# Two attentions of a fused block kernel: implied semaphore waits dropped, one wait moved, and products copied out 512 columns at a time

## The chip, the cores and the metric

The kernel runs on one core of one Trainium2 chip. The metric is the time on the device in microseconds (us) from one launch to its end. The engines are TensorE (PE, with its weight loads as PEld), VectorE (DVE), ScalarE (ACT), GpSimd (POOL) and the queue that issues the DMAs (SP). Each engine runs its own list of instructions in order, and they wait for each other by semaphores.

## The reference

Two layers follow each other on a sequence of 1024 tokens with 1024 features, all in float32. What the change touches is the two attentions, one in each layer:

```python
def one_block(qi):                       # first layer: 8 query heads, 2 key/value heads, width 64
    s = jnp.einsum('bqkgd,bskd->bkgqs', qi, k) * scale
    p = jax.nn.softmax(s, axis=-1)       # over all 1024 keys
    return jnp.einsum('bkgqs,bskd->bqkgd', p, v)

for blk in range(seqlen // ATT_BLOCK):   # second layer: 16 heads, width 64, causal
    q0, q1 = blk * ATT_BLOCK, (blk + 1) * ATT_BLOCK
    s = jnp.einsum('bhqd,bhkd->bhqk', q[:, :, q0:q1], k[:, :, :q1]) * scale
    s = s + fcum[:, :, q0:q1, None] - fcum[:, :, None, :q1]
    prob = jax.nn.softmax(jnp.where(kpos <= qpos, s, -jnp.inf), axis=-1)
    outs.append(jnp.einsum('bhqk,bhkd->bhqd', prob, v[:, :, :q1]))
```

Around them stand a gated token mixer, a gated feed-forward net with a short convolution, a state-space branch, and dense projections. Those are left as they are.

## The kernel before, in words

Every engine has a class with the same stages, and each stage walks the same steps, so that the order of an engine's work is the order of its own Python loop. A result is named by a label; `done(label)` lets the instruction raise its engine's one counter, and `wait_ge(*at(label))` waits for it. `wait_ge` leaves a wait out when this engine has already waited for a count of that semaphore at least as high (line 374 is where a wait is written, so every separate wait instruction has that line).

**One step of an attention.** The unit is a block of 128 queries of one head, numbered g. In the first attention there are 64 (eight heads of eight), and each sees 1024 keys. In the second there are 128: eight pairs p of heads with 16 blocks each, and block qt = g % 8 sees (qt + 1) * 128 keys. For one block the engines do this:

- PE `scores` (L805, L806): the query block against the high and the low part of the keys, 512 columns at a time into one of two PSUM tiles of 1024 columns. In the second attention a small matmul for the mask (L810) is last.
- DVE `top`: the maximum of each row (L2573); in the second attention a subtraction with maximum (L2568) and a change of sign (L2571, label `minus`).
- ACT `soft`: the exponential, with the row's sum (L1645). DVE `soft`: its reciprocal (L2581). POOL `weigh` (L3451, label `weighed`): the row times that reciprocal.
- PE `turn` (L829): transposes by 128 columns, four to a PSUM bank (bank 4 and bank 5). ACT `turn` (L1660, label `phi`) copies each bank out, rounded, as the high part; DVE `turn` (L2596, label `plo`) subtracts that from the bank and so makes the low part.
- PE `back` (L848), once for every two blocks (number n = g // 2): the values against the high and low parts, 256 columns, 16 matmuls in the first attention, into bank 6. Partitions 0 to 63 and 64 to 127 of the product are two partial sums. ACT `back` (L1668, label `outhi`) copies the first half out and DVE `back` (L2604, label `out`) adds the second to it.

**The order.** Step s of the first attention (s from -2 to 65) is, on PE: scores(s + 2), turn(s), and when s is even back(s - 1). On DVE: top(s + 2), the two subtractions of turn(s), reciprocal(s + 2), and when s is even the addition. On ACT: the two copies of turn(s), exponential(s + 2), and when s is even the copy of the product. On POOL: weigh(s + 2), and now and then an addition of squares. So "an even step" has a product at its end and "an odd step" has none.

In the second attention the steps are the same, but PE has other work between them. `self.fill(fills(p, s, True))` stands between scores(s + 2) and turn(s), and runs pieces of dense projections (three matmuls of 512 columns, L609 to L611, to a piece): none to three pieces a step. Their weights are split into a high part by ACT (L1393) and a low part by POOL (L3374), in POOL's one queue with `weigh`.

**Waits around the change.** `bank_free(b)` waits for the labels that the last user of bank b left in `emptied[b]`. For scores these are `top` and, in the first attention, `exp`; for the transposes `phi` and `plo` of the block that last used the bank; for the product `out`. PE waits for `weighed` of block g just ahead of the transposes of g, so in the second attention behind the pieces of dense work. At s == 22 of the first attention PE adds up the token mixer's squares into bank 7, and ACT takes the root.

Of the kernel before, what the change touches and what calls it, by code (L numbers as in the profile page):

```python
# [9 lines left out]
ACT = mybir.ActivationFunctionType  # L10
ALU = mybir.AluOpType
# [532 lines left out]


class TensorEngine(Engine):
    def __init__(self, K, op):
# [244 lines left out]

    def scores(self, A, g, h, qt, q, kh, kl, causal, ready):
        K = self.K
        nk = (qt + 1) * 128 if causal else 1024
        pair = g % 2
        qs = K.wrr(q)[:, qt * 128:(qt + 1) * 128]
        for half in range((nk + 511) // 512):
            c = slice(half * 512, min(nk, half * 512 + 512))
            out = K.ps[pair][:, c]  # L800
            diag = causal and c.stop == nk
            self.bank_free(2 * pair + half)
            for label in ready:
                self.wait_ge(*K.at(*label))
            self.op.matmul(out, qs, K.wrr(kh)[:, c], start=True, stop=False)  # L805
            t = self.op.matmul(out, qs, K.wrr(kl)[:, c], start=False, stop=not diag)  # L806
            if diag:
                self.consts()
                self.wait_ge(*K.at("maskr"))
                t = self.op.matmul(K.ps[pair][:, nk - 128:nk], K.idr[:, :], K.maskr[:, :],  # L810
                                   start=False, stop=True)
        t.then_inc(*self.done("scores", A, g))
        free = (("top", A, g),) if causal else (("top", A, g), ("exp", A, g))
        for half in range((nk + 511) // 512):
            self.emptied[2 * pair + half] = free

    def turn(self, A, g, qt, p, causal):
        K = self.K
        nk = qt + 1 if causal else 8
        par = g % 2 if nk <= 4 else 0  # L820
        self.consts()
        for half in range((nk + 3) // 4):
            bk = (half + par) % 2
            js = range(4 * half, min(nk, 4 * half + 4))
            self.wait_ge(*K.at("weighed", A, g))
            self.bank_free(4 + bk)
            for j in js:
                o = bk * 512 + (j - js[0]) * 128
                t = self.op.transpose(K.ps[2][:, o:o + 128], K.w(p)[:, j * 128:(j + 1) * 128],  # L829
                                      K.c_id)  # L830
            t.then_inc(*self.done("turn", A, g, half))
            self.emptied[4 + bk] = (("phi", A, g, half), ("plo", A, g, half))

    def back(self, A, g, qt, hi, lo, v, causal, ready):

        K = self.K
        nk = qt + 1 if causal else 8
        for gg in (g - 1, g):
            for half in range((((qt if gg == g else qt - 1) + 1 if causal else 8) + 3) // 4):
                self.wait_ge(*K.at("phi", A, gg, half))  # L840
                self.wait_ge(*K.at("plo", A, gg, half))
        for label in ready:
            self.wait_ge(*K.at(*label))
        self.bank_free(6)
        for j in range(nk):
            c0 = 128 if causal and j == qt else 0
            for n, m in enumerate((hi, lo)):
                t = self.op.matmul(K.ps[3][:, c0:256], K.wrr(v)[:, j * 128:(j + 1) * 128],  # L848
                                   m[:, j, c0:256], start=(j == 0 and n == 0),
                                   stop=(j == nk - 1 and n == 1))  # L850
        t.then_inc(*self.done("product", A, g // 2))
        self.emptied[6] = (("out", A, g // 2),)

    def attend1(self):
        K = self.K

        def sc(s):
            h, qt = s // 8, s % 8
            k = 8 if h < 4 else 10
            self.scores(1, s, h, qt, h, k, k + 1, False, (("stacklo", "q", h // 2), ("stacklo", "q", 4),  # L860
                         ("stackhi2", "q", 4, 1)))

        for s in range(-2, 66):
# [6 lines left out]
            if s >= 2 and s % 2 == 0:  # L870
                hi, lo, _ = pt1(K, ((s - 1) // 2) % 2)
                self.back(1, s - 1, (s - 1) % 8, hi, lo, 12 + (s - 1) // 32, False,
                          (("vstack", 1),))
            if s == 22:
                self.sums([22], [("toksq", 3)], 1, 3, "tok", 1)
            yield
# [344 lines left out]
    def attend2(self):  # L1221
        K = self.K
# [35 lines left out]
        for p in range(8):  # L1258
# [11 lines left out]
            def sc(s):  # L1270
# [3 lines left out]
                            (("stacklo", "q2", p, h), ("stacklo", "k", p, h),  # L1274
                             ("stackhi2", "k", p, h)))

# [99 lines left out]
class ScalarEngine(Engine):  # L1376
# [251 lines left out]
    def soft(self, A, g, qt, p, causal):  # L1628
# [3 lines left out]
        pw = K.w(p)[:, 0:nk]  # L1632
        self.wait_ge(*K.at("top", A, g))
        if causal:
            self.wait_ge(*K.at("minus", A, g))
        else:
            self.wait_ge(*K.at("scores", A, g))
            if g >= 4:
                for half in (0, 1):
                    self.wait_ge(*K.at("turn", A, g - 4, half))  # L1640
            else:
                self.wait_ge(*K.at("tok", 2 if g < 2 else 3))
        if g >= 16:
            self.wait_ge(*K.at("weighed", A, g - 16))
        self.op.activation(pw, pw if causal else K.ps[g % 2][:, 0:nk], ACT.Exp, bias=m, scale=1.0,  # L1645
# [17 lines left out]
    def back(self, A, g, h, qt, out):  # L1663
# [5 lines left out]
                           ACT.Copy).then_inc(*self.done("outhi", A, g // 2))  # L1669

    def attend1(self):
        K, w = self.K, self.K.w
        for s in range(-2, 66):
# [8 lines left out]
            if s >= 2 and s % 2 == 0:  # L1682
                h = (s - 1) // 8
                self.back(1, s - 1, h, (s - 1) % 8, K.htlf(4 + h // 2))
            if s in (4, 8, 12, 16):
# [5 lines left out]
                else:  # L1691
                    if j > 1:
                        self.wait_ge(*K.at("toksq", j - 1))
                    self.op.activation(w(23), w(14 + j),
                                       ACT.Square).then_inc(*self.done("toksq1", j))
            if s == 22:
                self.sqrt(3, 1, 1.0 / 512, K.eps, "tok", 1)
            if s in (36, 43, 50):
# [587 lines left out]
class VectorEngine(Engine):  # L2286
# [268 lines left out]
    def top(self, A, g, h, qt, p, causal):  # L2555
# [4 lines left out]
        self.wait_ge(*K.at("scores", A, g))  # L2560
        if g >= 16:
            self.wait_ge(*K.at("exp", A, g - 16))
        if causal:
# [11 lines left out]
    def soft(self, A, g):  # L2575
        K = self.K
        den, rd = (K.st[:, 4 * (g % 16) + j:4 * (g % 16) + j + 1] for j in (1, 2))
        self.wait_ge(*K.at("exp", A, g))
        if g >= 16:
            self.wait_ge(*K.at("weighed", A, g - 16))  # L2580
        self.op.reciprocal(rd, den).then_inc(*self.done("rd", A, g))  # L2581

    def turn(self, A, g, qt, parts, causal):
# [4 lines left out]
        for half in range((nk + 3) // 4):  # L2588
# [4 lines left out]
            r = slice(js[0], js[-1] + 1)  # L2593
            self.wait_ge(*K.at("turn", A, g, half))
            self.wait_ge(*K.at("phi", A, g, half))
# [3 lines left out]
    def back(self, A, g, h, qt, out):  # L2599
# [4 lines left out]
        self.op.tensor_tensor(out[a, c], K.ps[3][64:128, 0:256], out[a, c],  # L2604
                              ALU.add).then_inc(*self.done("out", A, g // 2))

    def attend1(self):
        K = self.K
        for s in range(-2, 66):
# [13 lines left out]
            if s >= 2 and s % 2 == 0:  # L2623
                h = (s - 1) // 8
                self.back(1, s - 1, h, (s - 1) % 8, K.htlf(4 + h // 2))
            if s == 22:
                self.reciprocal(8, "tok")
# [736 lines left out]
class GpSimd(Engine):  # L3364
# [78 lines left out]
    def weigh(self, A, g, qt, p, causal):  # L3443
# [4 lines left out]
        pw = K.w(p)[:, 0:nk]  # L3448
        self.wait_ge(*K.at("exp", A, g))
        self.wait_ge(*K.at("rd", A, g))  # L3450
# [902 lines left out]
```

## Time and profile before

| what | us |
|---|---|
| median of 3 runs (2622.33 to 2622.82) | 2622.48 |
| span of the profiled execution, first to last instruction | 2619.9 |
| PE busy, share of the span | 2539.2 (97%) |
| DVE busy | 1587.0 (61%) |
| ACT busy | 1233.5 (47%) |
| POOL busy | 1132.0 (43%) |
| mean granted TensorE clock | 0.991 |

The profiled execution's own time is its span and what lies around it: the median stands 2.6 us above the span. The first attention lies from about 256 to 470 us of the span, the second from about 1850 to 2346 us. A row of the timeline has the start, the duration, the engine, the line of the kernel, the operation, output <- inputs, and how many instructions are merged in it; in brackets stands the idle time of the engine before it and what ended that.

### The profile page before, as it was taken

The numbers are of one execution on the slowest core, as the hardware profiler recorded it, in microseconds if no ns is written. First come the engines' busy times: TensorE is split into PE (matmuls) and PEld (weight loads), VectorE is DVE, ScalarE is ACT, GpSimd is POOL, SyncE is SP. The second block draws the span as 40 slices with busy tenths as digits, with TensorE's granted clock in tenths as the row PEclk, the third lists the DMA queues.
The fourth block names the chain that finished last, engine by engine and source line by source line (L and its number), as shares of the span: only waits on it lengthen the run. The fifth ranks groups of instructions, "written<-read, shape, count | busy, mean of one in ns | idle before, by whom it ended". The sixth has DMA issues, their size and how long they took to land.

```text
span 2619.9 us, 33861 instructions
## 1 busy us (share of the span) xinstructions
PE 2539.2 (97%) x12946; PEld 2112.9 (81%) x12946; DVE 1587.0 (61%) x2413; ACT 1233.5 (47%) x1858; POOL 1132.0 (43%) x754
## 2 busy tenths in 40 slices
PE   5999999999999999999999999999999999999998
PEld 3788788777888888878788888888888888888886
DVE  7654889578555566575833366666666666655333
ACT  4343888445444443333533345543656656652132
POOL 0222434437878774444487334233322222235233
PEclk8999999999999999999999999999999999999999
DMA  6134000432222126553233322222111111157342
GB/s 271 65 121 129 1 1 1 142 101 83 94 77 92 73 100 226 192 177 109 107 113 121 121 73 89 81 69 93 57 53 53 49 49 57 60 206 279 146 185 97
DMA packets 84465, 275.89 MB, mean 105 GB/s; under 512 B 9392, under 2 KB 9520, under 8 KB 84304
## 3 DMA queue, kind: packets, MB, share of 16 engines
q1 hardware_dynamic: 84304, 273.71, 29.8%
q8 instruction: 104, 1.70, 0.3%
q14 instruction: 57, 0.47, 0.1%
HBM read 219.54 MB, written 54.13 MB: 104 GB/s over the span
## 4 chain that ended last, share of the span: by engine, by line
PE 81%; DVE 10%; ACT 5%; issue 2%; POOL 1%; DMA 0%; DVEq 0%; SPq 0%; ACTq 0%; POOLq 0%
PE ps L609 12%; PE ps L611 11%; PE ps L610 11%; PE ps L977 7%; PE ps L978 7%; PE ps L979 7%; PE ps L848 5%; PE ps L829 4%; PE ps L1034 3%; PE ps L1036 3%; PE ps L1035 3%; DVE wf L3047 2%; PE ps L805 2%; PE ps L806 2%; DVE st L2573 1%
## 5 line engine op out<-in xcount | busy, mean ns | idle before, releaser
L3374 POOL TENSOR_TENSOR hl<-raw,hl 128x1024 fp32r<-128x1024 f32 x161 | 403.6, 2509 | 929.9 <-ACT hl L1393 929.9
L609 PE MATMUL ps<-ht,hl 128*128 128x512 f32 x1552 | 633.7, 408 | 10.5 <-DVE ht L2444 5.4
L611 PE MATMUL ps<-ht,hl 128*128 128x512 f32 x1552 | 608.4, 392 | 0.0
L610 PE MATMUL ps<-ht,hl 128*128 128x512 f32 x1552 | 608.2, 392 | 0.0
L609 PEld LDWEIGHTS ps<-ht,hl 128*128 128x128 f32 x1552 | 293.6, 189 | 71.3 <-issue 6.2
L611 PEld LDWEIGHTS ps<-ht,hl 128*128 128x128 f32 x1552 | 293.0, 189 | 63.7
L610 PEld LDWEIGHTS ps<-ht,hl 128*128 128x128 f32 x1552 | 294.0, 189 | 54.2 <-issue 1.7
L3451 POOL TENSOR_SCALAR wf<-wf,st 128x1024 f32<-128x1024 f32 (+2 forms) x192 | 167.9, 874 | 343.1 <-DVE st L2581 287.4
L1393 ACT ACTIVATE hl<-raw 128x1024 fp32r<-128x1024 f32 x163 | 171.4, 1053 | 182.2 <-PE ps L1036 66.5
L2384 DVE TENSOR_TENSOR ps<-ps,wf 128x512 f32<-128x512 f32 x116 | 80.8, 697 | 152.1 <-PE ps L979 151.9
L829 PEld LDWEIGHTS ps<-cst,wf 128*128 128x128 f32 x1088 | 126.6, 141 | 56.2 <-issue 34.4
L829 PE MATMUL ps<-cst,wf 128*128 128x128 f32 x1088 | 157.5, 276 | 13.0 <-DVE ht L2596 12.7
L977 PE MATMUL ps<-wr,hl 128*128 128x512 f32 x384 | 149.7, 390 | 2.0 <-POOL hl L3502 1.4
L2596 DVE TENSOR_TENSOR wr<-ps,wr 128x512 fp32r<-128x512 f32 (+1 forms) x192 | 101.2, 555 | 79.9 <-ACT wr L1660 65.5
L979 PE MATMUL ps<-wr,hl 128*128 128x512 f32 x384 | 149.4, 389 | 0.0
L978 PE MATMUL ps<-wr,hl 128*128 128x512 f32 x384 | 149.4, 389 | 0.0
L1460 ACT ACTIVATE hl<-wf 128x512 fp32r<-128x512 f32 x97 | 60.5, 632 | 178.6 <-PE ps L979 132.3
L1034 PE MATMUL ps<-wr,hl 128*128 128x512 f32 x352 | 137.5, 391 | 3.3 <-POOL hl L3374 1.9
L2859 DVE TENSOR_TENSOR wr<-wf,wr 128x512 fp32r<-128x512 f32 x44 | 95.4, 2178 | 70.7 <-ACT wr L1855 70.6
L1036 PE MATMUL ps<-wr,hl 128*128 128x512 f32 x352 | 137.0, 389 | 0.0
L1035 PE MATMUL ps<-wr,hl 128*128 128x512 f32 x352 | 137.0, 389 | 0.0
L3502 POOL TENSOR_TENSOR hl<-wf,hl 128x512 fp32r<-128x512 f32 x97 | 128.6, 1347 | 14.4 <-ACT hl L1460 14.4
(287 smaller groups left out, 5298.5 us busy)
## 6 DMA issues: line engine op xcount, KB each, us to landing
raw<-in_wst SPq DMA_DIRECT2D x243, 512.0 KB, 4.0
wf<-scratch_rows SPq DMA_DIRECT2D x32, 512.0 KB, 5.0
scratch_g<-wf SPq DMA_DIRECT2D x22, 512.0 KB, 2.6
wf<-scratch_g SPq DMA_DIRECT2D x44, 256.0 KB, 4.4
wf<-in_xT SPq DMA_DIRECT2D x16, 512.0 KB, 8.0
htf<-in_wst SPq DMA_DIRECT2D x16, 512.0 KB, 15.4
scratch_ys<-wr SPq DMA_DIRECT2D x16, 512.0 KB, 4.8
ht<-scratch_ys SPq DMA_DIRECT2D x32, 256.0 KB, 6.0
```

The lines of the kernel that those rows point to most:

```text
L609: self.op.matmul(out, wh, xh[:, c], start=(j == 0), stop=False)
L610: self.op.matmul(out, wh, xl[:, c], start=False, stop=False)
L611: t = self.op.matmul(out, wl, xh[:, c], start=False, stop=(j == kt - 1))
L829: t = self.op.transpose(K.ps[2][:, o:o + 128], K.w(p)[:, j * 128:(j + 1) * 128], K.c_id)
L977: self.op.matmul(K.bank(bk), wh[:, c], xh, start=(j == 0), stop=False)
L978: self.op.matmul(K.bank(bk), wh[:, c], xl, start=False, stop=False)
L979: t = self.op.matmul(K.bank(bk), wl[:, c], xh, start=False, stop=(j == 3))
L1034: self.op.matmul(K.bank(n), wh, hi, start=(f == 0), stop=False)
L1035: self.op.matmul(K.bank(n), wh, lo, start=False, stop=False)
L1036: t = self.op.matmul(K.bank(n), wl, hi, start=False, stop=(f == NFF - 1))
L1393: self.op.activation(K.hl[:, u * 2048:u * 2048 + 1024], K.raw[:, i % 3 * 1024:(i % 3 + 1) * 1024], ACT.Copy).then_inc(*self.done("whi", i))
L3374: self.op.tensor_tensor(K.hl[:, u * 2048 + 1024:u * 2048 + 2048], K.raw[:, i % 3 * 1024:(i % 3 + 1) * 1024], hi.bitcast(F32), ALU.subtract ...
```

## The change

The first attention's product now goes to two banks by turns: products n = 0, 1 to the halves of bank 6, n = 2, 3 to those of bank 7, and so on. ACT copies and DVE adds only after every second product, 512 columns at a time; the last two products (n = 30, 31) are still taken singly with 256. Position in the order is unchanged: behind the second product of the two. The root of the token mixer's sums moves from step 22 to step 24 and to bank 6.

In both attentions waits are dropped that another wait implies, and the wait for `weighed` of block g - 2 is made inside `scores` of block g, ahead of its last matmul with the low part of the keys. As the transposes of block g - 2 come later in the same step, their own wait for it is then left out by `wait_ge`.

```diff
+def product_bank(A, g):
+    if A == 2:
+        return 6, 0
+    n = g // 2
+    return 6 + n // 2 % 2, n // 2 % 2 * 512 + n % 2 * 256
+
+def taken(g):
+    n = g // 2
+    if n >= 30:
+        return n, slice(n % 4 * 256, n % 4 * 256 + 256)
+    return (n - 1, slice((n - 1) % 4 * 256, (n - 1) % 4 * 256 + 512)) if n % 2 else None
...
     # TensorE
-    def scores(self, A, g, h, qt, q, kh, kl, causal, ready):
+    def scores(self, A, g, h, qt, q, kh, kl, causal, ready, weighed=None):
...
             self.op.matmul(out, qs, K.wrr(kh)[:, c], start=True, stop=False)
+            if c.stop == nk and weighed is not None:
+                self.wait_ge(*K.at("weighed", A, weighed))
             t = self.op.matmul(out, qs, K.wrr(kl)[:, c], start=False, stop=not diag)
...
-        free = (("top", A, g),) if causal else (("top", A, g), ("exp", A, g))
+        free = (("top", A, g),) if causal else (("exp", A, g),)
...
-            self.emptied[4 + bk] = (("phi", A, g, half), ("plo", A, g, half))
+            self.emptied[4 + bk] = (("plo", A, g, half),)
...
-                self.wait_ge(*K.at("phi", A, gg, half))
                 self.wait_ge(*K.at("plo", A, gg, half))
...
-        self.bank_free(6)
+        b, o = product_bank(A, g)
+        if o % 512 == 0:
+            self.bank_free(b)
...
-                         ("stackhi2", "q", 4, 1)))
+                         ("stackhi2", "q", 4, 1)), s - 2 if s >= 2 else None)
...
-            if s == 22:
-                self.sums([22], [("toksq", 3)], 1, 3, "tok", 1)
+            if s == 24:
+                self.sums([22], [("toksq", 3)], 1, 3, "tok", 0)
...
-                             ("stackhi2", "k", p, h)))
+                             ("stackhi2", "k", p, h)),
+                            16 * p + s - 2 if s >= 2 else None)
     # ScalarE: soft
-        self.wait_ge(*K.at("top", A, g))
         if causal:
             self.wait_ge(*K.at("minus", A, g))
         else:
-            self.wait_ge(*K.at("scores", A, g))
+            self.wait_ge(*K.at("top", A, g))
             if g >= 4:
-                for half in (0, 1):
-                    self.wait_ge(*K.at("turn", A, g - 4, half))
+                self.wait_ge(*K.at("turn", A, g - 4, 1))
...
-        if g >= 16:
-            self.wait_ge(*K.at("weighed", A, g - 16))
...
+    def back1(self, g, out):
+        K = self.K
+        n, c = taken(g)
+        h = g // 8
+        a = slice(64 * (h % 2), 64 * (h % 2) + 64)
+        o = product_bank(1, 2 * n)[1]
+        self.wait_ge(*K.at("product", 1, g // 2))
+        self.op.activation(out[a, c], K.ps[3][0:64, o:o + c.stop - c.start],
+                           ACT.Copy).then_inc(*self.done("outhi", 1, g // 2))
...
-                self.back(1, s - 1, h, (s - 1) % 8, K.htlf(4 + h // 2))
+                if taken(s - 1):
+                    self.back1(s - 1, K.htlf(4 + (s - 1) // 16))
     # VectorE: top, soft, turn; back1 is the addition of the same columns
-        if g >= 16:
-            self.wait_ge(*K.at("exp", A, g - 16))
...
-        if g >= 16:
-            self.wait_ge(*K.at("weighed", A, g - 16))
...
-            self.wait_ge(*K.at("turn", A, g, half))
             self.wait_ge(*K.at("phi", A, g, half))
...
     # GpSimd: weigh
-        self.wait_ge(*K.at("exp", A, g))
         self.wait_ge(*K.at("rd", A, g))
```

## Rows read from the trace of the kernel before

**Rows 1.** Busy time by stretch: the first attention, the second; then clock, DMA share, GB/s.
```profile
256.00:470.00 214.00, 197.65 (x1330) 167.53 (x1329) 182.82 (x296) 174.84 (x306) 85.10 (x70) 0.99 0.06 23
1840.00:2345.00 505.00, 502.60 (x2947) 431.67 (x2947) 327.05 (x835) 313.32 (x635) 156.27 (x155) 1.00 0.21 69
```

**Rows 2.** Timeline of one cycle, 412 to 417 us: DVE, ACT, PE, PEld.
```profile
414.19 0.43 DVE L2604 TENSOR_TENSOR htf<-ps,htf 64x256 f32<-64x256 f32 x1 [0.43 <-ACT htf L1668]
414.70 1.22 DVE L2573 TENSOR_REDUCE st<-ps 128x1 f32<-128x1024 f32 x1
...
413.78 0.38 ACT L1668 ACTIVATE htf<-ps 64x256 f32<-64x256 f32 x1 [0.22 <-PE ps L848]
...
414.27 0.39 PE L806 MATMUL ps<-wr 128*128 128x512 f32 x1
...
416.77 0.14 PEld L829 LDWEIGHTS ps<-cst,wf 128*128 128x128 f32 x1 [0.74 <-issue]
```

**Rows 3.** The chain of waits in the same cycle: start, duration, what.
```profile
415.80 0.17 issue
415.96 0.70 DVE ht L2596
416.66 0.14 issue
```

**Rows 4.** Prices by line and shape, 268 to 468 us: busy, mean ns, idle before.
```profile
L2596 DVE TENSOR_TENSOR ht<-ps,ht 128x512 fp32r<-128x512 f32 x128 | 82.2, 683 | 1.8 <-ACT ht L1660 1.3
...
L1660 ACT ACTIVATE ht<-ps 128x512 fp32r<-128x512 f32 x126 | 71.9, 597 | 26.4 <-PE ps L829 24.1
...
L2604 DVE TENSOR_TENSOR htf<-ps,htf 64x256 f32<-64x256 f32 x31 | 13.2, 427 | 8.9 <-ACT htf L1668 8.8
...
L1668 ACT ACTIVATE htf<-ps 64x256 f32<-64x256 f32 x32 | 12.0, 376 | 3.8 <-PE ps L848 2.4
```

**Rows 5.** Separate wait instructions (line 374), 415 to 417 us.
```profile
L374 DVEq EVENT_SEMAPHORE  x3: 21/21/21, 415.8 to 416.4; - x3
...
L374 PEldq EVENT_SEMAPHORE  x1: 51/51/51, 416.7 to 416.7; - x1
```

**Rows 6.** Timeline of DVE in another cycle, 289 to 290.2 us.
```profile
288.26 1.23 DVE L2573 TENSOR_REDUCE st<-ps 128x1 f32<-128x1024 f32 x1
289.41 1.28 DVE L2596 TENSOR_TENSOR ht<-ps,ht 128x512 fp32r<-128x512 f32 x2
```

**Rows 7.** Second attention, head pair 2: timeline of POOL, 1978 to 1998 us.
```profile
1979.28 2.39 POOL L3374 TENSOR_TENSOR hl<-raw,hl 128x1024 fp32r<-128x1024 f32 x1 [16.52 <-ACT hl L1393]
1981.64 0.38 POOL L3451 TENSOR_SCALAR wf<-wf,st 128x128 f32<-128x128 f32 x1
...
1989.38 2.40 POOL L3374 TENSOR_TENSOR hl<-raw,hl 128x1024 fp32r<-128x1024 f32 x1
1991.76 0.81 POOL L3451 TENSOR_SCALAR wf<-wf,st 128x640 f32<-128x640 f32 x1
...
1996.46 1.02 POOL L3451 TENSOR_SCALAR wf<-wf,st 128x896 f32<-128x896 f32 x1 [1.70 <-ACT wf L1668]
```

**Rows 8.** The same pair: timeline of PE, last low-part matmuls of three blocks' scores, and transposes.
```profile
1981.44 0.34 PE L806 MATMUL ps<-wr 128*128 128x384 f32 x1
...
1991.67 0.34 PE L806 MATMUL ps<-wr 128*128 128x384 f32 x1
...
1993.37 0.71 PE L829 MATMUL ps<-cst,wf 128*128 128x128 f32 x5
...
1997.31 0.27 PE L806 MATMUL ps<-wr 128*128 128x128 f32 x1
```

**Rows 9.** PE released by POOL, timeline 563 to 565 us.
```profile
561.94 2.38 POOL L3374 TENSOR_TENSOR hl<-raw,hl 128x1024 fp32r<-128x1024 f32 x1 [4.23 <-ACT hl L1393]
...
564.46 0.47 PE L609 MATMUL ps<-ht,hl 128*128 128x512 f32 x1 [1.26 <-POOL hl L3374]
```

**Rows 10.** The same pair: timeline of DVE, block 6's subtraction with maximum.
```profile
1993.61 1.07 DVE L2568 CUSTOM_DVE_ANT_0 wf<-ps,wf 128x896 f32<-128x896 f32 x1
```

More of the change, by code:

```diff
@@ L847, in back @@
             for n, m in enumerate((hi, lo)):
-                t = self.op.matmul(K.ps[3][:, c0:256], K.wrr(v)[:, j * 128:(j + 1) * 128],
+                t = self.op.matmul(K.ps[3][:, o + c0:o + 256], K.wrr(v)[:, j * 128:(j + 1) * 128],
                                    m[:, j, c0:256], start=(j == 0 and n == 0),
@@ L851, in back @@
         t.then_inc(*self.done("product", A, g // 2))
-        self.emptied[6] = (("out", A, g // 2),)
+        self.emptied[b] = (("out", A, g // 2),)
     def attend1(self):
@@ L1682, in attend1 @@
             if s >= 2 and s % 2 == 0:
-                h = (s - 1) // 8
-                self.back(1, s - 1, h, (s - 1) % 8, K.htlf(4 + h // 2))
+                if taken(s - 1):
+                    self.back1(s - 1, K.htlf(4 + (s - 1) // 16))
             if s in (4, 8, 12, 16):
@@ L1695, in attend1 @@
                                        ACT.Square).then_inc(*self.done("toksq1", j))
-            if s == 22:
-                self.sqrt(3, 1, 1.0 / 512, K.eps, "tok", 1)
+            if s == 24:
+                self.sqrt(3, 1, 1.0 / 512, K.eps, "tok", 0)
             if s in (36, 43, 50):
@@ L2605, in back, with back1 @@
                               ALU.add).then_inc(*self.done("out", A, g // 2))
+    def back1(self, g, out):
+        K = self.K
+        n, c = taken(g)
+        h = g // 8
+        a = slice(64 * (h % 2), 64 * (h % 2) + 64)
+        o = product_bank(1, 2 * n)[1]
+        self.wait_ge(*K.at("outhi", 1, g // 2))
+        self.op.tensor_tensor(out[a, c], K.ps[3][64:128, o:o + c.stop - c.start], out[a, c],
+                              ALU.add).then_inc(*self.done("out", 1, g // 2))
+        self.mark("out", 1, n)
     def attend1(self):
@@ L2623, in attend1 @@
             if s >= 2 and s % 2 == 0:
-                h = (s - 1) // 8
-                self.back(1, s - 1, h, (s - 1) % 8, K.htlf(4 + h // 2))
-            if s == 22:
+                if taken(s - 1):
+                    self.back1(s - 1, K.htlf(4 + (s - 1) // 16))
+            if s == 24:
                 self.reciprocal(8, "tok")
```

## The prediction

> **What bounds the kernel now.** I looked first at the busy time by stretch. In the second attention PE is busy for 502.6 of 505 us: nothing there can become faster by dropping waits, and every stall that is added to PE is paid in full. In the first attention PE is busy for 197.7 of 214 us, DVE for 182.8 and ACT for 174.8: no engine is full, so a chain that passes from engine to engine sets the time [rows 1].
>
> I then read that chain and laid the timeline beside it. One cycle is two blocks. PE runs the odd step's scores, whose last matmul starts at 414.27 and takes 0.39; DVE's maximum starts at 414.70, which is 0.04 after the end at 414.66 [rows 2]. The subtraction for the first four transposes follows at 415.96, and its end at 416.66 releases the even step's transposes [rows 3]; then come the product's 16 matmuls and the next odd scores. The next such maximum is 6.2 us later. The chain holds PE's three stages, the maximum and the subtraction. The copy of the product and the addition are not in it, though only just: the copy starts at 413.78, the addition ends at 414.19 + 0.43 = 414.62, and the maximum, which DVE runs next, starts 0.08 later [rows 2]. An instruction released late starts about 0.04 behind its releaser, so the addition could end some 0.05 later before it delayed the maximum.
>
> **First attention, the larger copy and addition.** A copy of 256 columns takes 0.376 and an addition 0.427; the same operations with 512 columns take 0.597 and 0.683 (these rows are of all 128 partitions; the ones in question have 64, and I take the time to follow the columns) [rows 4]. So the pair grows by 0.221 + 0.256 = 0.477. They stay between the product and the next odd maximum, so 0.477 - 0.05 = 0.43 us goes onto the chain. This happens 15 times (n = 1, 3, ..., 29): +6.4 us. Where the copy and addition are gone, in the 15 even n before 30, nothing is won: the maximum still waits for the scores at 414.66. Bounds: 0 if something else were late by as much, +7.2 if the 0.05 of slack is not there. The second bank brings nothing by itself: the addition ended at 414.62, 3 us before the next product is begun. I take +6.4.
>
> The Trainium skill ("Perfetto Trace Analysis", section "Optimizing Scalar/DVE Operations") says that grouping helps throughput where ScalarE or VectorE is saturated, and that where they are not but cause bubbles elsewhere, breaking instructions up may let work complete sooner. The trace has DVE at 182.8 of 214 us and PE waiting for it, so the second half of the rule applies, against this change; by the first half the sum would be a gain in DVE's busy time that here only becomes idle time.
>
> **First attention, waits dropped.** An instruction carries one wait; the others stand before it as instructions of their own [rows 5]. Two of them lie on the chain.
>
> On PE, the transposes waited for POOL (`weighed`), ACT (`phi`) and DVE (`plo`). The wait instruction of 0.051 is the last thing ahead of the weight load, which starts at 416.77, 0.11 after the subtraction's end at 416.66 [rows 2, 3, 5]. With `plo` alone, carried by the load itself, I expect the 0.04 of other releases: 0.07 won, and the same for the second four transposes, which are what the product follows. 31 cycles: -2.2 us.
>
> On DVE, the subtraction waited for PE and ACT. Its separate wait instruction is executed at 415.8, and the subtraction starts at 415.96, 0.03 after the maximum's end at 414.70 + 1.22 = 415.92 [rows 2, 5]. In other cycles it starts 1.15 after the maximum's start instead of 1.26, still overlapping its end [rows 6]. The two kinds of cycle differ by some 0.12, and I count 14 of the slow kind among 31. With one wait left, I expect the fast kind throughout: -1.6 us. Bounds for both together: 0 (the separate instructions cost nothing that the release doesn't cost) and -6 (31 x 0.19). I take -3.8.
>
> The other dropped waits, and the eight `phi` waits before a product, were met long before their instruction's turn and stand in front of queued work; the moved root stands in the same place two steps on. I put them at 0, with 1 us to either side. First attention: 6.4 - 3.8 = +2.6 us.
>
> The moved wait is harmless here. In a cycle `weigh` of two blocks before is done over half a us before it is asked for, and in the few cycles that the squares disturb, PE would wait for DVE's subtraction anyway.
>
> **Second attention, the moved wait.** Before, PE asked for `weighed` of block g - 2 just ahead of its transposes, behind up to three pieces of dense matmuls; now it asks ahead of the last low-part matmul of scores of block g, with those pieces queued behind the wait. PE has nothing to do meanwhile, and the pieces, the transposes and the next products all wait. I set the end of each `weigh` against the start of that matmul, by pair:
>
> - Block 0: POOL ends at 1981.64 + 0.38 = 1982.02, PE would start at 1981.44: late by 0.58. POOL was busy with a weight split of 2.39 until then.
> - Block 4: 1991.76 + 0.81 = 1992.57 against 1991.67: late by 0.90, again behind a split, of 2.40.
> - Block 6: 1996.46 + 1.02 = 1997.48 against 1997.31: late by 0.17.
>
> The rows are [rows 7, 8]. The other eleven blocks of the pair, set against each other in the same way, are in time by 0.25 or more. Before, all of this was hidden: the transposes of block 4 start only at 1993.37 [rows 8]. To each lateness comes the release: from POOL's end at 561.94 + 2.38 = 564.32 to the matmul at 564.46, 0.14 [rows 9]. That is 0.72, 1.04 and 0.31. A stall shifts PE, and what hangs on PE shifts too, so the second doesn't pay for the first. The third is smaller: block 6's maximum starts at 1993.61, long after its scores, because DVE is behind [rows 10], and is not delayed by the stall in them; only the step's transposes and copies are. I take 0.11 for it. A pair costs 1.87 us.
>
> The eight pairs repeat this. The first and the last differ in both directions and nearly cancel; I take 8 x 1.87 = 15.0 us. Bounds: 8 x (0.58 + 0.90) = 11.8 with neither release nor block 6, and 8 x (0.72 + 1.04 + 0.31 + 0.5) = 20.6 if the weight load of that matmul, which now can't run ahead, adds another 0.1 to 0.2 each time and nothing is given back. What is dropped here brings at most the 2.4 us in which PE is not busy, and more likely nothing.
>
> **The sum.** 2.6 + 15.0 = 17.6 us. The profiled span of 2619.9 becomes 2637.5; with the 2.6 us by which the median stands above it, 2640.1.
>
> **The rivals.**
>
> - *The addition is hidden* (0.15). The maximum is delayed by something of equal size anyway, so the 512 columns cost nothing and the dropped waits are won. For it: only a few tenths are in question. Against: the maximum follows both releasers by less than 0.1. Time: 2622.5 + 15.0 - 3.8 = 2633.7. By its effect on the sign it is the same case as the forecast.
> - *The moved wait is never met unready* (0.12, the other side). The place is the 23 or so waits for blocks 0, 4 and 6; it decides when POOL's `weigh` comes 0.6 and 0.9 us earlier relative to PE than it did. That would need the splits to stand elsewhere in POOL's time, since they are what delays it, or the exponential and the reciprocal to come sooner through their dropped waits. Against: the order of POOL is not changed, the split of 2.40 starts right behind the `weigh` before it, and on these blocks POOL is late because it is busy. Time: 2622.5 + 2.6 = 2625.1, and with the addition hidden too 2618.7. Within 0.2% most likely.
> - *Everything is dearer* (0.12). Each stall costs a weight load more, block 6 is paid in full, waits in time by only 0.25 are met as well, and the dropped waits bring nothing: 2622.5 + 20.6 + 7.2 = 2650.3.
> - The forecast as worked out: 0.61.
>
> **How the numbers follow.** The time is that of the likeliest case, 2640. The first and third rival and the bounds of both terms give about 2631 to 2650; beyond lie the second rival and a little of the third. I widen it slightly at the lower end, to 2629. About 0.2%, 5.2 us, is what a measurement of this kernel can tell from no change. Faster by more would need both attentions to go against me: 0.04. Within it lies most of the second rival: 0.08. Slower: 0.88.
>
> **What would show it.** In the second attention PE's busy time stays, the stretch grows by about 15 us, and the waits show PE or its weight loads at L806 released by POOL L3451, two or three times a pair, 0.6 to 1.2 us each. In the first, the odd maximum follows the addition by 0.03 in 15 cycles and the scores by 0.04 in the others; cycles with an addition last about 6.45, those without 6.0. The load at L829 follows the subtraction by about 0.04. The forecast is wrong if PE has no stall at L806, or if cycles with an addition are no longer than the others.

## The result, and the profile after

The changed kernel takes 2639.5 us (median of 4, 2636.8 to 2640.5), the one before 2622.4: a ratio of 1.0062, 95% interval 1.0048 to 1.0076. The forecast was 2640.0. The profiled execution has a span of 2638.5 us where 2637.5 was worked out. Lines of the changed kernel are numbered anew: scores L821 and L824 (were L805, L806), transposes L847 (L829), product L867 (L848), maximum L2597 (L2573), subtraction L2617 (L2596), copy of the product L1694 (L1668), addition L2635 (L2604), weighing L3482 (L3451). In the other kernels they differ from these by a few lines.

The busy time of the two attentions, to be set against [rows 1]:

```profile
256.00:472.40 216.40, 200.22 (x1333) 168.52 (x1331) 177.58 (x278) 169.96 (x289) 84.26 (x71) 0.99 0.05 19
1859.00:2364.10 505.10, 493.18 (x2891) 421.08 (x2890) 316.12 (x827) 300.04 (x623) 150.92 (x153) 1.00 0.19 64
```

In the second attention PE was busy for all but 2.4 of 505 us; now it is idle for 11.9, and the waits of that stretch name the reason:

```profile
PEld ps L824 <- POOL wf L3482: 16.0, 16, 1.4
...
PE ps L824 <- POOL wf L3482: 9.9, 15, 1.1
```

These are two stalls in each of the eight pairs. In pair 2, the timeline of POOL and PE shows blocks 0, 4 and 6, the ones of [rows 7, 8]:

```profile
1991.24 0.37 POOL L3482 TENSOR_SCALAR wf<-wf,st 128x128 f32<-128x128 f32 x1
...
1991.67 0.44 PE L824 MATMUL ps<-wr 128*128 128x384 f32 x1 [0.48 <-POOL wf L3482]
...
1991.95 0.22 PE L828 MATMUL ps<-maskr,idr 128*128 128x128 f32 x1
...
2002.07 0.81 POOL L3482 TENSOR_SCALAR wf<-wf,st 128x640 f32<-128x640 f32 x1
...
2002.93 0.45 PE L824 MATMUL ps<-wr 128*128 128x384 f32 x1 [0.76 <-POOL wf L3482]
...
2007.43 1.01 POOL L3482 TENSOR_SCALAR wf<-wf,st 128x896 f32<-128x896 f32 x1 [2.46 <-DVE st L2603]
...
2008.66 0.27 PE L824 MATMUL ps<-wr 128*128 128x128 f32 x1
```

The first matmul starts 0.06 after the weighing's end at 1991.61, the second 0.05 after 2002.88. Set against the usual distance from the matmul before them, the stalls are 0.64 and 0.92 us. Block 6 is weighed at 2008.44, in time for 2008.66.

Each stall has a smaller one behind it. The matmul that follows starts 0.28 us after the one that waited (1991.95 after 1991.67), as the weight load of the one that waited starts only with it, at 1991.66. In the kernel before it was 0.18 (1981.62 after the 1981.44 of [rows 8]):

```profile
1981.62 0.22 PE L810 MATMUL ps<-maskr,idr 128*128 128x128 f32 x1
```

With the two stalls of 0.64 and 0.92 and some 0.11 and 0.10 behind them a pair loses 1.78 us.

In the first attention, the timeline of DVE and the weight loads shows one cycle with an addition, to be set against [rows 2]:

```profile
290.23 1.22 DVE L2597 TENSOR_REDUCE st<-ps 128x1 f32<-128x1024 f32 x1 [0.80 <-PE ps L824]
291.37 1.28 DVE L2617 TENSOR_TENSOR ht<-ps,ht 128x512 fp32r<-128x512 f32 x2
...
295.94 0.69 DVE L2635 TENSOR_TENSOR htf<-ps,htf 64x512 f32<-64x512 f32 x1 [0.34 <-ACT htf L1694]
296.66 1.22 DVE L2597 TENSOR_REDUCE st<-ps 128x1 f32<-128x1024 f32 x1
```

```profile
292.11 0.42 PEld L847 LDWEIGHTS ps<-cst,wf 128*128 128x128 f32 x4 [0.55 <-DVE ht L2617]
```

The maximum at 290.23 follows the scores and has 0.80 us of idle VectorE ahead of it; the one at 296.66 follows the addition's end at 296.63 and is 6.43 us after it. The load at 292.11 is 0.05 behind the end of the first subtraction (two are merged in the row; one takes 0.68, and 291.37 + 0.68 = 292.05, before rounding 0.054), where it was 0.11 in [rows 2, 3]. The larger operations cost what their sort costs (the groups by shape, mean ns after the busy time), to be set against [rows 4]:

```profile
L2635 DVE TENSOR_TENSOR htf<-ps,htf 64x512 f32<-64x512 f32 x15 | 10.4, 694 | 5.6 <-ACT htf L1694 5.6
...
L1694 ACT ACTIVATE htf<-ps 64x512 f32<-64x512 f32 x15 | 8.9, 593 | 0.2
```

The length of each attention, from the start of its first scores matmul to the end of its last product matmul, is the measure of all that follows (us, from the one profiled execution of each kernel; the ratio is to the kernel before on the same chip):

| kernel | first | second | ratio, 95% interval |
|---|---|---|---|
| before | 211.8 | 492.7 | |
| changed | 214.8 | 504.9 | 1.0062 (1.0048 to 1.0076) |
| wait_back | 213.8 | 490.8 | 1.0002 (0.9994 to 1.0011) |
| no_512 | 209.9 | 504.9 | 1.0043 (1.0030 to 1.0055) |
| wait_only | 211.7 | 506.5 | 1.0049 (1.0035 to 1.0063) |
| only_512 | 216.5 | 492.9 | 1.0020 (1.0011 to 1.0028) |
| waits_dropped | 210.9 | 490.9 | 0.9989 (0.9980 to 0.9998) |
| copy_later | 213.9 | 490.9 | 1.0002 (0.9993 to 1.0011) |
| product_later | 212.3 | 490.9 | 0.9989 (0.9980 to 0.9998) |
| partitions_swapped | 210.0 | 490.8 | one execution |
| add_in_gap | 211.3 | 490.9 | 0.9992 (0.9983 to 1.0001) |
| product_filled | 209.0 | 490.9 | 0.9983 (0.9974 to 0.9992) |
| product_between | 221.1 | 490.8 | 1.0032 (1.0019 to 1.0044) |
| between_free | 206.5 | 490.8 | 0.9981 (0.9972 to 0.9990) |

Up to 1 us of a difference between two first attentions in this table belongs to a single cycle near 270 us, between the odd maxima of blocks 3 and 5, in which TensorE's granted clock differs from execution to execution. The busy times and the clock of 264 to 280 us, for wait_back and for waits_dropped:

```profile
264.00:280.00 16.00, 12.65 (x84) 10.07 (x83) 13.34 (x20) 13.89 (x22) 4.95 (x5) 1.00 0.00 1
264.00:280.00 16.00, 13.99 (x79) 12.50 (x80) 13.33 (x22) 12.13 (x22) 4.50 (x5) 0.79 0.00 1
```

The length of the cycle goes with that clock. At a mean of 1.00 (all of it at the higher level, 2.4 GHz) that cycle lasts 5.99 us, at 0.79 (a part at the lower one, 1.2 GHz) 7.93; in the kernel before, the changed one and no_512 the mean is 0.89 and the cycle 6.89 to 7.02. Without that cycle, kernels with the same code there agree to 0.02 us: the kernel before and wait_only 204.8, the changed one and wait_back 207.8, no_512 and waits_dropped 203.0; only_512 has 209.5.

The rest of the program differs by up to some 4 us between executions of one kernel. One source is seen in the changed kernel's trace: in a stretch of dense work that no edit touches, the mean granted clock was 0.57 for 3.6 us, which is the lower level for most of them, and 1.00 at the same work in the kernel before. TensorE was busy throughout, and for 4.23 of the 4.40 us ahead of it too.

```profile
1257.50:1261.10 3.60, 3.60 (x13) 2.97 (x13) 1.61 (x7) 0.56 (x2) 0.00 (x0) 0.57 0.10 37
```

Matmuls of 512 columns follow each other by 0.43 us in it and by 0.23 behind it, so it costs some 1.6 us (my estimate: 8 of them at 0.20). Seven of the fourteen executions profiled have such a stretch there, whatever their edits.

The two profiled spans differ by 18.6 us, 15.2 of them in the attentions (2.95 and 12.25). That leaves 3.4 us of the spans outside them. Of the 17.1 us between the medians it leaves 1.9 that I don't explain; the clock in that stretch can be a part of them.

### The profile page after: what moved, and what is told of

The parts are those of the page before. It is cut to its first block, busy times and chain, and to the rows that moved or that the text cites. A ratio compares the mean times of both kernels' runs of the same rounds, so it can differ in the third digit from the quotient of the medians.

```text
span 2638.5 us, 32712 instructions
## 1 busy us (share of the span) xinstructions
PE 2546.4 (97%) x12946; PEld 2116.7 (80%) x12946; DVE 1582.6 (60%) x2398; ACT 1228.0 (47%) x1843; POOL 1131.5 (43%) x754
## 4 chain that ended last, share of the span: by engine, by line
PE 77%; DVE 10%; ACT 8%; POOL 3%; issue 1%; DMA 0%; SPq 0%; DVEq 0%; ACTq 0%; POOLq 0%
PE ps L625 11%; PE ps L627 11%; PE ps L626 11%; PE ps L996 7%; PE ps L998 7%; PE ps L997 7%; PE ps L867 4%; PE ps L847 3%; PE ps L1053 3%; PE ps L1055 3%; PE ps L1054 3%; DVE wf L3079 2%; POOL hl L3406 2%; PE ps L824 2%; DVE st L2597 1%
## 5 line engine op out<-in xcount | busy, mean ns | idle before, releaser
L3482 POOL TENSOR_SCALAR wf<-wf,st 128x1024 f32<-128x1024 f32 (+2 forms) x192 | 167.7, 874 | 355.5 <-DVE st L2603 355.4
L847 PE MATMUL ps<-cst,wf 128*128 128x128 f32 x1088 | 158.2, 277 | 14.4 <-DVE ht L2617 12.7
L847 PEld LDWEIGHTS ps<-cst,wf 128*128 128x128 f32 x1088 | 127.1, 141 | 55.4 <-DVE ht L2617 32.3
L2617 DVE TENSOR_TENSOR wr<-ps,wr 128x512 fp32r<-128x512 f32 (+1 forms) x192 | 100.6, 552 | 91.0 <-ACT wr L1676 90.8
L1676 ACT ACTIVATE wr<-ps 128x512 fp32r<-128x512 f32 (+1 forms) x192 | 87.2, 490 | 109.8 <-PE ps L847 109.5
```

## The experiments

**The moved wait, taken back.**

```diff
-                             ("stackhi2", "k", p, h)),
-                            16 * p + s - 2 if s >= 2 else None)
+                             ("stackhi2", "k", p, h)))
```

> The changed kernel, but in the second attention TensorE asks for `weighed` ahead of the transposes again, behind the dense pieces. Theory (the moved wait makes the loss there): the two stalls of a pair at the last low-part matmul go, 8 x 1.53 = 12.2 us, so about 2627 us, and a pair lasts 63.07 us again. Rival (the loss comes from the other edits there, such as waits dropped elsewhere that now let engines run in another order): stays near 2639 us with pairs of 64.6 us.

The second attention fell from 504.9 to 490.8 us, by 14.1 where 12.2 was expected: I had left out the 0.21 a pair behind the stalls, and 8 x 1.78 = 14.2. Pairs last 62.84 us, 0.23 less than before the change. All of the loss there was the moved wait, and the dropped waits win 1.85 us in all, which I had put at nothing. The gain lies ahead of TensorE's weight loads: in that stretch the loader stands idle for 6.2 us before loads of the transposes and 3.2 before those of the products in the kernel before, and for 4.7 and 2.8 here. The whole is level with the kernel before.

**The moved wait alone.**

```diff
...
+            if c.stop == nk and weighed is not None:
+                self.wait_ge(*K.at("weighed", A, weighed))
...
+                            16 * p + s - 2 if s >= 2 else None)
```

> The kernel before with one edit: in the second attention the wait for `weighed` is made in the scores. Theory: +12.2 us, 2634.6 us, stalls of about 0.64 and 0.92 us in blocks 0 and 4 of each pair. Rival (the stalls need the dropped waits beside it, or are absorbed): 2622 to 2624 us.

The second attention grew by 13.8 us, with stalls of 0.63 and 0.93 in blocks 0 and 4 of pairs 1 to 6. The rival falls. The 12.25 of the changed kernel are its moved wait, 14.1, less the 1.85.

**The 512 columns, without and alone.** The first is the changed kernel with `back` in place of `back1`, the second the kernel before with the two new functions and `back1`.

```diff
...
-                if taken(s - 1):                              # no_512, from the changed kernel
-                    self.back1(s - 1, K.htlf(4 + (s - 1) // 16))
+                self.back(1, s - 1, h, (s - 1) % 8, K.htlf(4 + h // 2))
```

> The changed kernel, but each product of the first attention is copied and added by itself again, 256 columns in bank 6, with the root back at step 22. Theory: the first attention shrinks from 214.8 to about 209.8 us, 2 us below what it was in the kernel before, because only the separate wait of TensorE (0.06 a cycle) is won: 2634.5 us. On the slow kind of cycle two accounts differ: if the separate wait instruction of VectorE made it slow (my step in the prediction), all cycles last 6.01 us and the first attention 208.3; if it is the addition that works on partitions 64 to 127 and keeps a later instruction from overlapping, the cycles of the odd heads stay 0.12 longer than those of the even heads.

```diff
...
-                self.back(1, s - 1, h, (s - 1) % 8, K.htlf(4 + h // 2))
+                if taken(s - 1):                              # only_512, from the kernel before
+                    self.back1(s - 1, K.htlf(4 + (s - 1) // 16))
...
```

> The kernel before with one edit: products in two banks, copied and added 512 columns at a time. Theory: a cycle with an addition is 0.42 us longer, 15 x 0.42 = 6.3 us, less some 0.8 us where cycles of odd heads now have no addition: first attention 217.3 us instead of 211.8, 2628 us. Rival (the larger size is hidden or saves engine time): 2621 to 2622.5 us.

Alone, the larger copies made the first attention 4.7 us longer; cycles of the even heads last 6.50 with an addition and 6.07 without, exactly the 0.43 forecast. It is 4.7 and not the 6.4 of 15 such cycles for two reasons. In the odd heads a cycle with an addition and one without together grew by 0.34. And the three cycles around the root, one of them with an addition, went from 21.28 us to 20.64 in all; I don't know why. Without the larger copies the changed kernel's first attention is 209.9, 1.9 us below the kernel before. The cycles settled the dispute over VectorE's wait. In no_512 the separate wait instruction is gone (VectorE has 2 in the first attention, where it had 177), and still the odd heads' cycles last 6.13 and the even heads' 6.01. The timeline of its DVE, an even head's cycle and an odd head's:

```profile
289.56 1.23 DVE L2594 TENSOR_REDUCE st<-ps 128x1 f32<-128x1024 f32 x1
290.70 0.68 DVE L2614 TENSOR_TENSOR ht<-ps,ht 128x512 fp32r<-128x512 f32 x1
...
307.76 1.22 DVE L2594 TENSOR_REDUCE st<-ps 128x1 f32<-128x1024 f32 x1
309.02 0.69 DVE L2614 TENSOR_TENSOR ht<-ps,ht 128x512 fp32r<-128x512 f32 x1
```

The subtraction starts 1.14 after the maximum's start in the one and 1.26 in the other.

**The partitions swapped.** It is the kernel waits_dropped, further below, but even heads go to partitions 64 to 127 and odd ones to 0 to 63, so the heads stand in each other's place in its result.

```diff
         a = slice(64 * (h % 2), 64 * (h % 2) + 64)
+        if A == 1:
+            a = slice(64 - a.start, 128 - a.start)
```

> The kernel waits_dropped with the two halves of the partitions swapped in the first attention's copy and addition, so that even heads go to partitions 64 to 127 and odd heads to 0 to 63 (the heads are swapped in the result). Theory (an addition on partitions 64 to 127 keeps the subtraction behind the maximum from overlapping it): the late subtractions, 0.03 behind the maximum's end, move from the odd heads' cycles to the even heads', the rest start 0.08 before its end. Rival (they belong to the odd heads' data or to the place in the loop): they stay with the odd heads.

The late subtractions moved: the timeline of DVE shows a cycle of the loop's first head (head 0, an even one) and one of the next.

```profile
287.82 1.23 DVE L2595 TENSOR_REDUCE st<-ps 128x1 f32<-128x1024 f32 x1
289.08 1.29 DVE L2615 TENSOR_TENSOR ht<-ps,ht 128x512 fp32r<-128x512 f32 x2
...
306.10 1.22 DVE L2595 TENSOR_REDUCE st<-ps 128x1 f32<-128x1024 f32 x1
307.24 1.28 DVE L2615 TENSOR_TENSOR ht<-ps,ht 128x512 fp32r<-128x512 f32 x2
```

Now the even head has the late start (1.26 after the maximum's) and the odd one the early one (1.14). So it is the partitions of the addition two instructions earlier, 0.11 us a cycle, and not the wait. (ScalarE's copy was swapped with it; the late start is VectorE's own, behind its own maximum.)

**The dropped waits by themselves.**

It is no_512 with wait_back's edit as well:

```diff
-                             ("stackhi2", "k", p, h)),
-                            16 * p + s - 2 if s >= 2 else None)
+                             ("stackhi2", "k", p, h)))
...
```

> The changed kernel without the larger copies and with the wait for `weighed` of the second attention back ahead of the transposes: what is left are the dropped waits, and the moved wait in the first attention. Theory: first attention 209.9 us (1.9 below the kernel before), pairs of the second 62.84 us (1.85 us in all), ratio 0.9986, about 3.8 us faster. Rival (the dropped waits gain nothing by themselves and the two stretches only moved by chance): within 1 us of the kernel before.

Ratio 0.9989, 0.9980 to 0.9998: about 2.9 us faster, where 3.8 was expected and lies inside the interval. In the two attentions it is 0.86 and 1.79 us, and without the cycle near 270 us 1.8 each. It is the part of the change worth keeping.

**The larger addition elsewhere.** Both kernels have wait_back's waits.

```diff
-            if s >= 2 and s % 2 == 0:            # copy_later, on ACT and DVE
+            if s >= 3 and s % 2 == 1 and s < 63 or s in (62, 64):
...
+            if s >= 4 and s % 2 == 0 and s <= 62 and taken(s - 3):     # add_in_gap, on DVE
```

> The changed kernel with the second attention's wait back ahead of the transposes, and with the 512-column copy and addition one step later on ScalarE and VectorE (behind the odd step's reciprocal; the last two products stay where they are). Theory (the place ahead of the odd maximum makes the larger addition dear, not its size): cycles with an addition fall from 6.43 to 6.01 and none starts its subtraction late, first attention about 208.3 us, 2617 us in all. Rival (512 columns cost wherever they stand, since VectorE is 85% busy): first attention 213 to 215 us, 2624 us.

This theory fell: 213.9 us, as the rival had it (without the cycle near 270 us 207.0, where wait_back has 207.8, so the new place won little). The timeline of DVE in a cycle with an addition:

```profile
284.25 0.17 DVE L2603 RECIPROCAL st<-st 128x1 f32<-128x1 f32 x1 [0.23 <-ACT wf L1660]
284.71 0.69 DVE L2635 TENSOR_TENSOR htf<-ps,htf 64x512 f32<-64x512 f32 x1 [0.30 <-ACT htf L1693]
285.44 1.23 DVE L2597 TENSOR_REDUCE st<-ps 128x1 f32<-128x1024 f32 x1
```

and of ACT:

```profile
284.10 0.58 ACT L1693 ACTIVATE htf<-ps 64x512 f32<-64x512 f32 x1
...
286.70 1.12 ACT L1660 ACTIVATE wf<-ps,st 128x1024 f32<-128x1024 f32 x1 [1.06 <-DVE st L2597]
```

The even maximum could have followed the reciprocal at once. Behind the copy and the addition it starts 1.1 us later, the exponential waits for it, the reciprocal waits for that, and the next odd maximum comes 0.43 after its scores. A second chain (maximum, exponential, reciprocal, maximum) lies just under the first.

> The kernel copy_later with the 512-column addition moved once more, to the even step behind that step's reciprocal, where VectorE waited about 1 us for the scores of the odd step; its copy is done by then. Theory (an addition is free only where VectorE waits for TensorE, and only if it fits: 0.69 us into the 0.9 to 1.0 us): every undisturbed cycle lasts 6.0 us, no subtraction starts late in the odd heads, first attention 208 to 209 us, some 3 to 5 us faster than the kernel before. Rival (two additions' worth of work costs its time wherever it stands): first attention stays at 213 to 215 us and the whole within 1 us of the kernel before.

Between the two: cycles with an addition last 6.13 in the even heads and 6.39 in the odd ones, against 6.01 without. Many of the odd heads' cycles without an addition last 6.13, behind one with it. The 0.69 us don't quite fit into the gap of VectorE. The first attention is 211.3 us.

**The product elsewhere.** From waits_dropped on, with 256 columns.

```diff
-            if s >= 2 and s % 2 == 0:            # product_later: PE behind turn(s), ACT, DVE
+            if s >= 3 and s % 2 == 1:
...
-            if s >= 3 and s % 2 == 1:            # product_between: PE between scores and turn
+            if s % 2 == 0 and 4 <= s <= 62:
```

> The kernel waits_dropped with product, copy and addition (256 columns) of the first attention all one step later: TensorE multiplies behind the odd step's transposes instead of ahead of the odd scores. Theory (the chain runs through the 16 matmuls of the product because they stand between the even transposes and the odd scores): TensorE does them in the time in which it waited for the subtraction, the cycle falls from 6.01 to what VectorE and TensorE need, 5.7 to 5.9, so the first attention is 202 to 206 us and the whole 2612 to 2616 us, faster than both kernels. Rival (the wait only moves to the transposes or VectorE is full): 208 us or more, 2618 us.

```diff
-        self.op.activation(out[a, c], K.ps[3][0:64, 0:256],     # product_filled, beside that
+        self.op.activation(out[a, c], K.ps[3][0:64, o:o + 256],   # two banks by turns
...
-            if s >= 2 and s % 2 == 0:            # copy on ACT, at even steps
+            g = s - 3 if s % 2 == 0 and 4 <= s <= 62 else s - 2 if s in (63, 65) else -1
...
+            if s % 2 == 1 and 5 <= s <= 63:      # addition on DVE, at odd steps, of g = s - 4
```

> The kernel product_later with each product in its own bank by turns, its copy one step later behind the exponential, and its addition two steps later between the subtractions and the reciprocal of an odd step. (The root goes to bank 6, and one square of the norm two steps later.) Theory (product_later was held by the exchange of VectorE and ScalarE, maximum, exponential, reciprocal, next maximum, with the addition in it; out of it, the cycle is what TensorE needs, 5.7 us): cycles of 5.7 to 5.8, first attention 201 to 204 us, the whole about 9 us faster than the kernel before. Rival (VectorE is full and the exchange stays the bound whatever stands in it): cycles of 6.0 to 6.2 as in product_later, first attention 209 to 212 us.

The cycles of product_later last 5.93 to 6.44, most of them 6.13 or more, and those of product_filled 6.01 where undisturbed and up to 6.44 elsewhere (the first two cycles and those around the root left out, in both). Both rivals held. Moving the product from the even to the odd transposes only let the chain run over the even maximum: in product_filled it goes from that maximum (1.22 us) over a subtraction, the odd transposes (1.25) and the product (1.91) to the even scores and the next even maximum. product_filled is 0.9983 of the kernel before.

> The kernel product_filled with TensorE's product moved from behind the odd step's transposes to between the next even step's scores and its transposes. Theory (in product_later and product_filled the product still stood between transposes and the next scores, so the chain went on through its 16 matmuls, only over the even maximum; between scores and transposes it fills the time in which TensorE waits for the maximum and the subtraction of the same step): the chain of a cycle no longer holds the product's 2.0 us, TensorE's own work of 5.7 us bounds it, cycles of 5.7 to 5.8, first attention 200 to 203 us, ratio about 0.995. Rival (VectorE and ScalarE's exchange bounds at 6.0): cycles stay at 6.0, first attention 208 to 210 us, ratio 0.998.

Neither: 221.1 us, cycles of 6.53. The chain of waits shows what I had not counted:

```profile
406.33 1.13 POOL wf L3487
407.47 0.04 issue
407.51 0.50 PE ps L822
408.01 1.92 PE ps L865 x16
409.93 0.45 PE ps L845 x4
```

The moved wait stands in the scores, and the product is queued behind it. The weighing now comes late, and everything in the chain waits for it.

```diff
-                         ("stackhi2", "q", 4, 1)), s - 2 if s >= 2 else None)
+                         ("stackhi2", "q", 4, 1)))    # between_free, beside product_between
```

> The kernel product_between without the moved wait in the first attention too: TensorE asks for `weighed` ahead of the transposes, behind the product. Theory (product_between lost because its chain ran from the weighing over the wait in the even scores into the product, 314 ns of stall ahead of the last low-part matmul and then 16 matmuls behind it): the product covers the weighing, cycles fall from 6.53 to 5.7 to 5.9, first attention 201 to 206 us, ratio 0.995 to 0.997. Rival (the product between scores and transposes delays the transposes by itself, whatever is waited for): cycles stay above 6.3, first attention 215 us or more, ratio above 1.0.

Without the moved wait the first attention falls from 221.1 to 206.5 us, the shortest of all, though still above the 201 to 206 expected. Its chain again has the product in some cycles and VectorE's own work in the others:

```profile
404.66 1.12 DVE st L2599
405.78 1.20 DVE ht L2619 x2
...
407.01 0.43 DVE htf L2628
407.44 0.03 issue
407.47 0.16 DVE st L2605
407.63 0.03 issue
407.66 1.23 DVE st L2599
408.88 0.68 DVE ht L2619
409.56 0.14 issue
409.70 1.16 PE ps L845 x8
```

Cycles are 5.93 where undisturbed, not 5.7 to 5.9: VectorE is full for much of them. In all it is 0.9981 of the kernel before (0.9972 to 0.9990) and 0.8% below the changed kernel by the medians (of two chips), faster than both, though not clear of product_filled. The expected 0.995 to 0.997 was missed.

## Why the prediction was right, and which terms were off

- **The second attention pays for every stall.** Right in place and count. The forecast was 15.0 us, measured 12.25. The moved wait alone cost 14.1. The lateness carried over as worked out: 0.58 and 0.90 of [rows 7, 8] became stalls of 0.64 and 0.92 with the release in them. The release was mis-sized at 0.14, it measured 0.05 to 0.06, because [rows 9] have a separate wait instruction in it and this wait is carried by the load. Block 6 cost nothing, not 0.11. The weight load that can't run ahead, which I had only in the upper bound, cost 0.21 a pair. The dropped waits, put at nothing, won 1.85; that is most of the 2.75 by which the term was too high.
- **The larger copy and addition.** 0.43 a cycle was right in the even heads (6.50 against 6.07). In the odd heads two cycles grew from 12.40 to 12.74, 0.34, since a cycle without an addition is free of the late subtraction. Alone it cost 4.7 us, not 6.4: some 0.6 of the 1.7 lie in the odd heads and 1.1 in the cycles around the root, which stays open.
- **The wait instruction on TensorE.** Right: forecast 0.07 a cycle, measured 0.06 (load 0.116 behind the subtraction before, 0.054 after), 1.9 us over 31 cycles against 2.2.
- **The wait instruction on VectorE.** The step failed. I took two kinds of cycle for the price of a wait: "With one wait left, I expect the fast kind throughout: -1.6 us." The wait went and the slow kind stayed; it follows the partitions of the addition. No run shows a price for that wait: without it the two kinds of cycle became 0.06 and 0.07 us shorter, which the load on TensorE accounts for.
- **The moved wait in the first attention.** Put at nothing. In the changed kernel it was met unready four times there, 1.6 us in all, and yet in no_512, which has it too, no cycle is more than 0.01 us longer than in the kernel before. No run takes it back there alone, with the product in its old place.
- **First attention in all.** +2.6 forecast, +2.95 measured, from terms of +6.4 - 3.8 that were really +4.7 - 1.8: errors of 1.7 and 2.0 us that nearly cancelled. That the sum came out is luck.
- **Of the rivals,** none came. The addition is not hidden, the moved wait is met unready 16 times, not some 23, and nothing was dearer. The 1.9 us outside the attentions made up for most of the overestimate in the second, which is luck as well; without them the time would have been about 2637.6. The range and the direction don't rest on it.

## What to carry to other kernels

A wait moved earlier in an in-order queue takes everything between its old and new place with it: before moving one, set the end of the awaited work against the new place, block by block, above all where dense work stood in between. One wait fewer ahead of an instruction on the chain is worth some hundredths of a microsecond; merging two small operations into one large one can cost more than that where both stand on a chain between engines that aren't full. Before an operation is moved off the chain, look for the next chain below it: here the product taken off the first chain won 0.08 us a cycle (6.01 to 5.93), and the larger addition moved from the first to the second still cost 0.40 (6.01 to 6.41).

## What the hardware showed that I had not expected

A VectorE instruction may start 0.08 us before the end of the one ahead of it, or 0.03 after, and which of the two it is can depend on partitions. With the addition at partitions 64 to 127, the subtraction behind the next maximum starts 0.03 after the maximum's end; with 0 to 63 it starts 0.08 before it. This followed the partitions when they were swapped. The Trainium skill ("VectorE: DVE Perf Modes", section "Two Vector instructions with no wait between them") gives a model by which an instruction is held until all earlier ones are finished, when one of its inputs starts in another quadrant (a group of 32 partitions) than the first input that the last instruction to read the same memory took from it. The trace agrees with that: the maximum reads PSUM alone, so the last instruction that read SBUF before the subtraction is the addition, whose SBUF input starts at partition 64 in every other head. Its PSUM input starts there in all heads, and the maximum right behind it starts 0.03 after its end even in an even head (296.66 above). Here the subtraction waits for a semaphore as well and the hold is there all the same; its price was some 0.115 us (1.26 against 1.14 after the maximum's start).
